# A two-layer token mixer on one core: in the delta rule's scan, two pairs of small products on TensorE are issued alternately, each pair in PSUM banks of its own, and ScalarE's copies stand in another order

## The chip, the cores and the metric

The kernel runs on one core of one Trainium2 chip, written in Bass: each engine (TensorE, VectorE, ScalarE, GpSimd, and SyncE for the DMAs) has its own instruction stream, and they are held together by semaphores that are written out by hand. The metric is the device time of one execution in microseconds (us). The kernel before has a median of 2457.78 us of 3 runs (2455.46 to 2459.18).

## What is computed

A trunk of two layers over 256 context tokens and 1024 latent tokens of width 1024. The even layer mixes an mLSTM branch and an RWKV-7 branch, the odd one an HGRN-2 branch and a long convolution. The change touches one function alone, the scan of the RWKV-7 branch, which runs in both directions over all 1280 tokens, with 8 heads of dimension 64. Cut to that part, the reference is:

```
def rwkv_scan(inputs, S):
    def step(S, xs):
        r, v, kk, w, k, a = xs
        sa = jnp.einsum('bhvk,bhk->bhv', S, -kk)
        S = S * w[:, :, None, :] + sa[..., None] * (kk * a)[:, :, None, :] + v[..., None] * k[:, :, None, :]
        return S, jnp.einsum('bhvk,bhk->bhv', S, r)

    S, ys = lax.scan(step, S, tuple(jnp.moveaxis(t, 2, 0) for t in inputs))
    return jnp.moveaxis(ys, 0, 2), S
```

## The kernel before

The scan (`stage_rwkv_scan`, from L1540) does not go token by token. It takes chunks of 64 tokens (C), 20 for each direction, 40 in all (N). Within a chunk the delta rule is a triangular system; its matrix is inverted by doubling, and the state passes from chunk to chunk. A **round** b (20 of them, B) inverts the matrices of the two chunks 2b and 2b+1, called lanes 0 and 1, and in the gaps of that work it carries the state through the two chunks of round b-1 and prepares those of round b+1. The 8 heads lie as 4 pairs (j), a pair's two heads (q) on the lower and the upper 64 partitions.

**The inversion** has five levels n (TOP = 5). Each is a ring through four engines' steps:

- `half_product(b, n)` (L1831, TensorE, 16 products of 64x64) into the pair banks 0 and 1; it waits for `merge_upper(b, n-1)`.
- `copy_half(b, n)` (L1901, ScalarE) copies the two banks to SBUF.
- `upper_product(b, n)` (L1840, TensorE, 16 products) waits for that copy and for `turn_inverse(b, n)` (L2045, L2047, VectorE, three 32x32 block transposes).
- `merge_upper(b, n)` (L2052, VectorE, a predicated copy of both banks) puts the result into the inverse, and then the next level's `half_product` may start.

While TensorE waits for a step of another engine, it does the work of the other rounds that its program puts there. In level 1 this is `begin_chunk(b-1, 0)` (L1787: the state times the first queries) and `strict_products(b+1, 0)` (L1730) ahead of the upper product, `solve_chunk(b-1, 0)` (L1796) and `begin_outputs(b-1, 0)` (L1805) behind it. Level 2 has `update` (L1813) and `end_outputs` (L1819) of lane 0 ahead, and `products(b+1, 0)` (L1741) behind. Levels 3 and 4 do the same for lane 1, with `begin_outputs` ahead of `solve_chunk`. Level 5 has `pull(b)` (L1778: both lanes, values times a part of the products) ahead, and `turn_keys` (L1753) and `turn_v` (L1768, transposes) behind.

All these products except `products`, `update`, `end_outputs` and the transposes use a quarter of TensorE: 64 rows by 64 columns. `strict_products`, `begin_chunk` and `solve_chunk` alternate between the two quarters in which rows and result lie in the same half (q, q); `pull` and `begin_outputs` use the two others. The half and upper products go through all four.

PSUM's eight banks in the scan: 0 and 1 the inversion, 2 and 5 the turned keys of the lanes, 3 and 4 `products` (4 also `turn_v`), 5 also `strict_products`, 6 (CHAIN) `pull`, `begin_chunk`, `solve_chunk` and `update`, 7 the outputs.

ScalarE's own order in a round is: `copy_keys` (L1905) of both lanes, half 1, values (L1912), outputs of two chunks back (L1941), u of lane 0 (L1924), half 2, values, strict of lane 0 (L1932, from bank 5 to `strict_t`), half 3, outputs, u of lane 1, strict of lane 1, half 4, half 5, `copy_pulled` (L1919). An engine takes its instructions in this order, whichever is ready first. `update` waits for the copied u, and `begin_chunk` for the copied pull.

GpSimd starts the next round's inverses (`begin_inverse`, L1988) from VectorE's masked products (`read_products`, L2037), and adds the second direction's outputs (L2000). SyncE loads the operands two rounds ahead, and weights of the next stage.

Of the kernel before, what the change touches and what calls it, by code (L numbers as in the profile page):

```python
# [19 lines left out]
P = 128  # L20
# [1519 lines left out]
def stage_rwkv_scan(p, arena, operands, v_dram, shared, spare, own, chunk_decay, y, next_weights, free, bonus_dram):  # L1540
# [55 lines left out]
    with ExitStack() as local:  # L1596
# [23 lines left out]
        PAIR, KEYS, TURN, STRICT, CHAIN, OUT = 0, (2, 5), 3, 5, 6, 7  # L1620
# [11 lines left out]
        with nc.Block() as block:  # L1632
# [88 lines left out]
            def _(pe):  # L1721
                def strict_products(b, lane):
                    s = 2 * b + lane
                    pe.wait_ge(operands_loaded[s % SLOTS], landed(s))
                    if s:
                        pe.wait_ge(strict_read, s)
                    if lane == 0 and b >= 2:
                        pe.wait_ge(keys_copied, 2 * (b - 1))
                    for j, q in both:
                        last = nc.tensor.matmul(bank(STRICT)[part(q), at(lane, j)], queries(s)[part(q), j, q, :],  # L1730
                                                keys(s)[part(q), j, q, :], start=True, stop=True)
                    last.then_inc(strict_ready, 1)

                def products(b, lane):
                    s = 2 * b + lane
                    if s:
# [8 lines left out]
                def turn_keys(b):  # L1745
                    for lane in range(2):
                        s = 2 * b + lane
                        if lane == 0 and b:
                            pe.wait_ge(keys_copied, 2 * b - 1)
                        if lane == 1:  # L1750
                            pe.wait_ge(strict_read, min(2 * (b + 2), N))
                        for j in range(J):
                            last = nc.tensor.transpose(bank(KEYS[lane])[:, j * P:(j + 1) * P],  # L1753
                                                       keys(s)[:, j].rearrange("p k t -> p (k t)"), p.const("ident"))
                        last.then_inc(keys_turned, 1)
# [16 lines left out]
                def pull(b):  # L1772
                    if b < WINDOWS:
                        pe.wait_ge(v_copied, 2 * (b + 1))
                    pe.wait_ge(state_ready, 2 * b + 1)
                    for lane in range(2):
                        for j, q in both:
                            last = nc.tensor.matmul(bank(CHAIN)[part(q), at(lane, j)], prod[part(1 - q), b % 2, lane, q, j, part(q)],  # L1778
                                                    uv(2 * b + lane)[part(1 - q), q, j, :], start=True, stop=True)
                    last.then_inc(pulled_ready, 1)  # L1780

# [9 lines left out]
                def solve_chunk(b, lane):  # L1791
                    s = 2 * b + lane
                    pe.wait_ge(rest_copied, s + 1)
                    pe.wait_ge(upper_merged, TOP * (b + 1))
                    for j, q in both:
                        last = nc.tensor.matmul(bank(CHAIN)[part(q), at(1, j)], own_inverse(b, lane, j, q), rest[part(q), j, :],  # L1796
                                                start=True, stop=True)
                    last.then_inc(u_summed, 1)

                def begin_outputs(b, lane):  # L1800
                    s = 2 * b + lane
                    if s:
                        pe.wait_ge(y_copied, s)
                    for j, q in both:
                        nc.tensor.matmul(bank(OUT)[part(1 - q), at(0, j)], queries(s)[part(q), j, 1 - q, :], state[part(q), j, :],  # L1805
                                         start=(j == 0), stop=False)
# [37 lines left out]
                for lane in range(2):  # L1844
                    strict_products(0, lane)
                    products(0, lane)
                turn_v(0)
                for b in range(B):
# [4 lines left out]
                    if ahead:  # L1853
                        strict_products(b + 1, 0)
                    upper_product(b, 1)
                    if before:
                        solve_chunk(b - 1, 0)
                        begin_outputs(b - 1, 0)
# [8 lines left out]
                    if ahead:  # L1867
                        strict_products(b + 1, 1)
                    if before:
                        begin_chunk(b - 1, 1)  # L1870
                    upper_product(b, 3)
                    if before:
                        begin_outputs(b - 1, 1)
                        solve_chunk(b - 1, 1)
# [8 lines left out]
                    pull(b)  # L1883
                    upper_product(b, 5)
                    turn_keys(b)
                    if b + 1 < WINDOWS:
                        turn_v(b + 1)
                for lane in range(2):
                    begin_chunk(B - 1, lane)
                    solve_chunk(B - 1, lane)  # L1890
                    begin_outputs(B - 1, lane)
                    update(B - 1, lane)
                    end_outputs(B - 1, lane)

            @block.scalar
            def _(act):
# [18 lines left out]
                def copy_pulled(b):  # L1915
                    act.wait_ge(pulled_ready, b + 1)
                    if b:
                        act.wait_ge(rest_copied, 2 * b)
                    nc.scalar.copy(flat(pulled[:, :, :, :]), narrow(bank(CHAIN))).then_inc(pulled_copied, 1)  # L1919
# [25 lines left out]
                for b in range(B):  # L1945
# [6 lines left out]
                    if b >= 2:  # L1952
                        copy_y(b - 2, 1)
# [7 lines left out]
                    if before:  # L1961
                        copy_y(b - 1, 0)
                        copy_u(b - 1, 1)
                    if ahead:
                        copy_strict(b + 1, 1)
                    copy_half(b, 4)
                    copy_half(b, 5)
# [3 lines left out]
                copy_y(B - 2, 1)  # L1971
# [1981 lines left out]
```

## Time and profile before

| | |
|---|---|
| median of 3 runs | 2457.78 us |
| span of the profiled execution | 2456.0 us (the median lies 1.8 us above it) |
| TensorE busy over the span | 2299.8 us, 94% |
| VectorE, ScalarE, GpSimd busy | 1340.4, 814.9, 250.8 us |
| the scan: first half product to last upper product | 926.5 to 1302.3 us |
| instruction queue of the whole kernel | 175 packets, 2.87 MB |

A profile page gives each engine's busy time, the groups of instructions by line and the chain that ended last. TensorE's records need care: each fp32 product of 64x64 stands in the trace as two LDWEIGHTS and two MATMUL records, so a group of 8 products shows as x16 and one of 16 as x32. A record's duration (some 0.22 us) is much longer than the distance to the next one, since products in different quarters overlap; what a group takes from TensorE is the distance from its first start to the first start of the next group. "issue" names idle time in which the engine waited for nothing that the profile shows.

### The profile page before, as it was taken

The numbers are of one execution on the slowest core, as the hardware profiler recorded it, in microseconds if no ns is written. First come the engines' busy times: TensorE is split into PE (matmuls) and PEld (weight loads), VectorE is DVE, ScalarE is ACT, GpSimd is POOL, SyncE is SP. The second block draws the span as 40 slices with busy tenths as digits, with TensorE's granted clock in tenths as the row PEclk, the third lists the DMA queues.
The fourth block names the chain that finished last, engine by engine and source line by source line (L and its number), as shares of the span: only waits on it lengthen the run. The fifth ranks groups of instructions, "written<-read, shape, count | busy, mean of one in ns | idle before, by whom it ended". The sixth has DMA issues, their size and how long they took to land. (4 is left out here: it accounts for less than half of the span.)

```text
span 2456.0 us, 50670 instructions
## 1 busy us (share of the span) xinstructions
PE 2299.8 (94%) x22140; PEld 1419.3 (58%) x22140; DVE 1340.4 (55%) x2181; ACT 814.9 (33%) x1533; POOL 250.8 (10%) x280
## 2 busy tenths in 40 slices
PE   6999999999989988988887998999998999999898
PEld 4444456666644447887784443444685666756443
DVE  3320335553348757777884454555395666667514
ACT  4121222224445653443342222110101445465311
POOL 0000000000002211111221102341100000000000
PEclk8999999999989999999998998999999999999999
DMA  8100122122055654433325432111122100000233
GB/s 332 60 19 7 43 78 76 63 65 71 22 154 144 170 155 117 118 91 93 96 58 194 128 109 76 47 47 34 69 102 82 36 27 27 27 18 10 96 97 116
DMA packets 131867, 207.29 MB, mean 84 GB/s; under 512 B 15630, under 2 KB 95246, under 8 KB 128063
## 3 DMA queue, kind: packets, MB, share of 16 engines
q1 hardware_dynamic: 118398, 154.74, 20.2%
q0 software_dynamic: 13248, 49.32, 7.0%
q8 instruction: 175, 2.87, 0.5%
q14 instruction: 46, 0.37, 0.0%
HBM read 154.01 MB, written 50.01 MB: 83 GB/s over the span
## 5 line engine op out<-in xcount | busy, mean ns | idle before, releaser
L737 PE MATMUL psum<-arena,shared 128*128 128x512 f32 (+1 forms) x864 | 328.7, 525 | 1.5 <-PEq L223 1.5
L2858 PE MATMUL psum<-arena,second_shared 128*128 128x512 f32 (+1 forms) x640 | 282.4, 568 | 11.0 <-PEq L3679 6.4
L737 PEld LDWEIGHTS psum<-arena,shared 128*128 128x128 f32 x864 | 157.0, 191 | 108.8 <-issue 101.8
L2858 PEld LDWEIGHTS psum<-arena,second_shared 128*128 128x128 f32 x640 | 112.5, 195 | 77.0 <-issue 71.8
L1243 PE MATMUL psum<-shared,arena 128*128 128x512 f32 x320 | 150.0, 617 | 0.0
L2244 PE MATMUL psum<-shared,fin_mix 128*128 128x512 f32 x320 | 143.4, 601 | 3.0 <-POOL fin_mix L2377 3.0
L1901 ACT COPY r_half<-psum 128x512 f32<-128x512 f32 x100 | 58.6, 586 | 151.1 <-PE psum L1831 151.0
L2244 PEld LDWEIGHTS psum<-shared,fin_mix 128*128 128x128 f32 x320 | 59.8, 192 | 75.0 <-issue 71.5
L1243 PEld LDWEIGHTS psum<-shared,arena 128*128 128x128 f32 x320 | 60.3, 196 | 73.4 <-issue 72.9
L841 ACT ACTIVATE shared<-psum 128x512 f32<-128x512 f32 (+1 forms) x48 | 25.2, 524 | 216.4 <-PE psum L737 216.4
L2052 DVE COPY_PREDICATED r_inv<-shared,psum 128x512 f32<-128x512 uint32 x100 | 73.4, 734 | 42.9 <-PE psum L1840 42.0
L2047 DVE STREAM_TRANSPOSE r_lower<-r_inv 64x256 f32<-64x256 f32 x200 | 88.0, 440 | 2.7
L1831 PE MATMUL psum<-r_inv,r_strict_t 64*64 64x64 f32 x3200 | 75.6, 226 | 14.2 <-issue 6.1
L1988 POOL TENSOR_TENSOR r_inv<-r_prod,shared 64x256 f32<-64x256 f32 x80 | 57.9, 724 | 289.1 <-PE psum L1796 188.5
L330 PE MATMUL psum<-arena,shared 128*128 128x512 f32 (+3 forms) x240 | 87.4, 523 | 0.0
L3143 DVE TENSOR_TENSOR arena<-arena,g_k 128x512 f32<-128x512 f32 x56 | 39.5, 706 | 87.4 <-ACT arena L3011 87.4
L1840 PE MATMUL psum<-r_half,r_lower 64*64 64x64 f32 x3200 | 75.3, 224 | 12.2 <-issue 8.9
L3011 ACT ACTIVATE arena<-arena 128x1024 f32<-128x1024 f32 x64 | 69.3, 1083 | 34.5 <-DVE arena L3124 32.8
L2849 PE MATMUL psum<-second_shared,arena 128*128 128x128 f32 x640 | 80.3, 277 | 0.0
L1831 PEld LDWEIGHTS psum<-r_inv,r_strict_t 64*64 64x64 f32 x3200 | 60.3, 135 | 29.0 <-issue 14.3
L2849 PEld LDWEIGHTS psum<-second_shared,arena 128*128 128x128 f32 x640 | 75.1, 192 | 1.1 <-issue 0.5
L3429 PE MATMUL psum<-arena,yf_weight 128*128 128x512 f32 x168 | 74.4, 592 | 0.0
(457 smaller groups left out, 4231.8 us busy)
## 6 DMA issues: line engine op xcount, KB each, us to landing
arena<-scratch_operands SPq DMA_DIRECT2D x152, 128.0 KB, 2.7
shared<-in_l_w_in SPq DMA_DIRECT2D x22, 512.0 KB, 4.0
scratch_spill<-shared POOLq DMA_DIRECT2D x16, 640.0 KB, 3.2
second_shared<-in_l_w_in SPq DMA_DIRECT2D x20, 512.0 KB, 3.8
scratch_operands<-arena POOLq DMA_DIRECT2D x14, 640.0 KB, 8.3
scratch_operands<-arena POOLq DMA_DIRECT2D x28, 320.0 KB, 11.2
shared<-in_l_mod_w SPq DMA_DIRECT2D x8, 1024.0 KB, 9.1
t_matrix<-in_transform SPq DMA_DIRECT2D x8, 1024.0 KB, 5.0
```

Of the source, the lines that this page charges most:

```text
L330: last = nc.tensor.matmul(p.psum[0:rows_out, bank_of[u], 0:width], lhsT, rhs, start=(k == 0), stop=(k == KT - 1))
L737: last = nc.tensor.matmul(p.psum[:, FILL + f % BANKS, 0:width], weight[:, q % PIECES, k, :], hT[:, k, at:at + width], start=(k == 0), stop ...
L1243: last = nc.tensor.matmul(p.psum[:, PROJECT + u % 2, :], hT[:, k, t * P:(t + 1) * P], weight[:, job, k, :], start=(k == 0), stop=(k == KT ...
L1831: last = nc.tensor.matmul(pair_bank(q, lane, jj)[part(r)], strict_t[part(q), b % 2, lane, 2 * jj + r, :], own_inverse(b, lane, 2 * jj + r, ...
L1840: last = nc.tensor.matmul(pair_bank(q ^ r, lane, jj)[part(q)], lower[part(r), q ^ r, four(lane, jj), :], half[part(r), q, four(lane, jj), ...
L2047: last = nc.vector.transpose(lower[part(1 - q), 1], here[part(q), 1])
L2052: nc.vector.copy_predicated(inv[:, b % 2].rearrange("p s l j n -> p s (l j) n"), added_to_pairs(direction(b), n), pair_banks.rearrange("p ...
L2244: last = nc.tensor.matmul(p.psum[:, OUT + 2 * (t % 2) + n, :], mixed[:, t % SLOTS, k, :], weight[:, k, n * BANK:(n + 1) * BANK], start=(k ...
L2849: last = nc.tensor.matmul(bank[:, (t - part[0]) * P:(t - part[0] + 1) * P], hT[:, kk, t * P:(t + 1) * P], w[:, kk, :], start=(kk == 0), st ...
L2858: last = nc.tensor.matmul(bank[:, 0:width], w[:, kk, :], hT[:, kk, first:first + width], start=(kk == 0), stop=(kk == KT - 1))
L3011: nc.scalar.activation(out, out, ACT.Exp).then_inc(sig["exps_ready"], 1)
L3429: last = nc.tensor.matmul(bank(made), left[:, k, :], right[:, k, :], start=(k == 0), stop=(k == HALF - 1))
```

## The change

Only `stage_rwkv_scan` is changed, in TensorE's and ScalarE's programs.

- `pull` gets bank 2 (PULL) in place of CHAIN, and the two keys' banks swap lanes. It is cut in lanes. `strict_and_pull(b, lane)` issues, for each pair of heads, two strict products of round b+1 and two pull products of round b in turn. Lane 0's stands in level 3, lane 1's in level 5, both between the half and the upper product. The strict products therefore leave level 1 (lane 0) and level 3 (lane 1), and half of the pull leaves level 5.
- `solve_and_begin_outputs` issues two products of the solve and two of the outputs' beginning in turn, in levels 1 and 3, behind the upper product.
- `turn_keys` is called by lanes, with `turn_v` between them; lane 1 waits for `copy_pulled`, whose bank it shares.
- The wait for the landed operands moves from the strict products to `products`, which is now the first reader.
- ScalarE: the copy of the outputs of lane 1 moves from the next round's level 1 to behind half 4; the strict copy of lane 1 moves from ahead of half 4 to behind half 5. The strict copy of lane 0 stays where it was, ahead of half 3. `copy_pulled` waits for both lanes' pulls and reads bank 2.

```diff
-        PAIR, KEYS, TURN, STRICT, CHAIN, OUT = 0, (2, 5), 3, 5, 6, 7
+        PAIR, KEYS, PULL, TURN, STRICT, CHAIN, OUT = 0, (5, 2), 2, 3, 5, 6, 7
...
+                def strict_and_pull(b, lane):
+                    if b + 1 < B:
+                        await_strict(b + 1, lane)
+                    if b < WINDOWS:
+                        pe.wait_ge(v_copied, 2 * b + lane + 1)
+                    if lane == 0 and b:
+                        pe.wait_ge(keys_copied, 2 * b)
+                    for j in range(J):
+                        if b + 1 < B:
+                            strict_product(2 * (b + 1) + lane, j, 0)
+                            strict = strict_product(2 * (b + 1) + lane, j, 1)
+                        pull_product(2 * b + lane, j, 1)
+                        pull = pull_product(2 * b + lane, j, 0)
+                    if b + 1 < B:
+                        strict.then_inc(strict_ready, 1)
+                    pull.then_inc(pulled_ready, 1)
...
-                def solve_chunk(b, lane):
+                def solve_and_begin_outputs(b, lane):
                     s = 2 * b + lane
                     pe.wait_ge(rest_copied, s + 1)
                     pe.wait_ge(upper_merged, TOP * (b + 1))
...
+                    for j in range(J):
+                        for q in range(2):
+                            last = nc.tensor.matmul(bank(CHAIN)[part(q), at(1, j)], own_inverse(b, lane, j, q), rest[part(q), j, :],
+                                                    start=True, stop=True)
+                        for q in (1, 0):
+                            nc.tensor.matmul(bank(OUT)[part(1 - q), at(0, j)], queries(s)[part(q), j, 1 - q, :], state[part(q), j, :],
+                                             start=(j == 0), stop=False)
+                    last.then_inc(u_summed, 1)
...
                     half_product(b, 1)
                     if before:
                         begin_chunk(b - 1, 0)
-                    if ahead:
-                        strict_products(b + 1, 0)
                     upper_product(b, 1)
                     if before:
-                        solve_chunk(b - 1, 0)
-                        begin_outputs(b - 1, 0)
+                        solve_and_begin_outputs(b - 1, 0)
...
                     half_product(b, 3)
-                    if ahead:
-                        strict_products(b + 1, 1)
                     if before:
                         begin_chunk(b - 1, 1)
+                    strict_and_pull(b, 0)
                     upper_product(b, 3)
                     if before:
-                        begin_outputs(b - 1, 1)
-                        solve_chunk(b - 1, 1)
+                        solve_and_begin_outputs(b - 1, 1)
...
                     half_product(b, 5)
-                    pull(b)
+                    strict_and_pull(b, 1)
                     upper_product(b, 5)
-                    turn_keys(b)
+                    turn_keys(b, 0)
                     if b + 1 < WINDOWS:
                         turn_v(b + 1)
+                    turn_keys(b, 1)
...
                     copy_half(b, 1)
                     copy_v(b, 0)
-                    if b >= 2:
-                        copy_y(b - 2, 1)
                     if before:
                         copy_u(b - 1, 0)
                     copy_half(b, 2)
...
                         copy_y(b - 1, 0)
                         copy_u(b - 1, 1)
+                    copy_half(b, 4)
+                    if before:
+                        copy_y(b - 1, 1)
+                    copy_half(b, 5)
                     if ahead:
                         copy_strict(b + 1, 1)
-                    copy_half(b, 4)
-                    copy_half(b, 5)
                     copy_pulled(b)
```

How the instructions stand now. TensorE, level 3 of a round and the start of level 4, before (L1831 half product, L1730 strict, L1787 begin_chunk, L1840 upper, L1805 outputs' beginning, L1796 solve):

```order
L1831 MATMUL psum<-r_inv,r_strict_t 64x64 x16
L1730 MATMUL psum<-arena 64x64 x8
L1787 MATMUL psum<-r_state,arena 64x64 x8
L1840 MATMUL psum<-r_half,r_lower 64x64 x16
L1805 MATMUL psum<-r_state,arena 64x64 x8
L1796 MATMUL psum<-r_rest,r_inv 64x64 x8
L1831 MATMUL psum<-r_inv,r_strict_t 64x64 x16
```

The same place in the changed kernel (L1845 half product, L1803 begin_chunk, L1723 strict, L1727 pull, L1854 upper, L1815 solve, L1818 outputs' beginning); the pairs of rows at L1723 and L1727, and those at L1815 and L1818, come four times each:

```order
L1845 MATMUL psum<-r_inv,r_strict_t 64x64 x16
L1803 MATMUL psum<-r_state,arena 64x64 x8
L1723 MATMUL psum<-arena 64x64 x2
L1727 MATMUL psum<-shared,r_prod 64x64 x2
...
L1854 MATMUL psum<-r_half,r_lower 64x64 x16
L1815 MATMUL psum<-r_rest,r_inv 64x64 x2
L1818 MATMUL psum<-r_state,arena 64x64 x2
```

The strict products of level 3 are now the next round's lane 0, where they were lane 1, and they stand behind begin_chunk, where they stood ahead of it.

ScalarE, from half 2 to the copy of the pull, before (L1901 half, L1912 values, L1932 strict, L1941 outputs, L1924 u, L1919 pulled):

```order
L1901 COPY r_half<-psum 128x512
L1912 COPY r_uv<-psum 64x256 x2
L1932 COPY r_strict_t<-psum 128x256
L1901 COPY r_half<-psum 128x512
L1941 COPY r_y<-psum 128x256
L1924 COPY r_uv<-psum 64x256 x2
L1932 COPY r_strict_t<-psum 128x256
L1901 COPY r_half<-psum 128x512 x2
L1919 COPY r_pulled<-psum 128x512
```

And now (L1910 half, L1921 values, L1941 strict, L1950 outputs, L1933 u, L1928 pulled):

```order
L1910 COPY r_half<-psum 128x512
L1921 COPY r_uv<-psum 64x256 x2
L1941 COPY r_strict_t<-psum 128x256
L1910 COPY r_half<-psum 128x512
L1950 COPY r_y<-psum 128x256
L1933 COPY r_uv<-psum 64x256 x2
L1910 COPY r_half<-psum 128x512
L1950 COPY r_y<-psum 128x256
L1910 COPY r_half<-psum 128x512
L1941 COPY r_strict_t<-psum 128x256
L1928 COPY r_pulled<-psum 128x512
```

The first strict copy keeps its place between half 2 and half 3, the second has moved behind half 5, and a copy of outputs stands between half 4 and half 5.

## Rows read from the trace of the kernel before

**Rows 1.** The page: the span and section 1, busy time by engine.
```profile
span 2456.0 us, 50670 instructions
...
PE 2299.8 (94%) x22140; PEld 1419.3 (58%) x22140; DVE 1340.4 (55%) x2181; ACT 814.9 (33%) x1533; POOL 250.8 (10%) x280
```

**Rows 2.** Busy time in stretches: start:end, length, busy us of PE, PEld, DVE, ACT, POOL, clock, DMA.
```profile
945.00:1300.00 355.00, 315.78 (x10960) 287.16 (x10957) 283.69 (x561) 147.42 (x334) 64.54 (x89) 1.00 0.33 91
```

**Rows 3.** Timeline of TensorE, one round: start, length, engine, line, count, idle before.
```profile
1040.08 0.69 PE L1831 MATMUL psum<-r_inv,r_strict_t 64*64 64x64 f32 x32
...
1047.50 0.69 PE L1831 MATMUL psum<-r_inv,r_strict_t 64*64 64x64 f32 x32
1048.01 0.63 PE L1730 MATMUL psum<-arena 64*64 64x64 f32 x16
1048.48 0.63 PE L1787 MATMUL psum<-r_state,arena 64*64 64x64 f32 x16
1048.99 0.69 PE L1840 MATMUL psum<-r_half,r_lower 64*64 64x64 f32 x32
1049.52 0.46 PE L1805 MATMUL psum<-r_state,arena 64*64 64x64 f32 x10
...
1050.53 0.69 PE L1831 MATMUL psum<-r_inv,r_strict_t 64*64 64x64 f32 x32
1051.39 0.69 PE L1813 MATMUL psum<-shared,r_k_tok 128*64 128x64 f32 x16 [0.17 <-ACT shared L1924]
...
1054.62 0.69 PE L1831 MATMUL psum<-r_inv,r_strict_t 64*64 64x64 f32 x32
1055.15 0.63 PE L1778 MATMUL psum<-shared,r_prod 64*64 64x64 f32 x16
1055.62 0.63 PE L1778 MATMUL psum<-r_uv,r_prod 64*64 64x64 f32 x16
1056.12 0.99 PE L1840 MATMUL psum<-r_half,r_lower 64*64 64x64 f32 x32
...
1058.50 0.69 PE L1831 MATMUL psum<-r_inv,r_strict_t 64*64 64x64 f32 x32
```

**Rows 4.** Timeline of ScalarE in levels 3 and 4 of the same round.
```profile
1048.26 0.58 ACT L1901 COPY r_half<-psum 128x512 f32<-128x512 f32 x1 [2.48 <-PE psum L1831]
1048.74 0.38 ACT L1941 COPY r_y<-psum 128x256 f32<-128x256 f32 x1
1050.50 0.75 ACT L1924 COPY shared<-psum 64x256 f32<-64x256 f32 x2 [1.38 <-PE psum L1796]
1051.27 0.37 ACT L1932 COPY r_strict_t<-psum 128x256 f32<-128x256 f32 x1
1051.54 0.59 ACT L1901 COPY r_half<-psum 128x512 f32<-128x512 f32 x1
```

**Rows 5.** Timeline of VectorE, the merge in level 3 of the same round.
```profile
1049.74 0.73 DVE L2052 COPY_PREDICATED r_inv<-shared,psum 128x512 f32<-128x512 uint32 x1
```

**Rows 6.** DMA queues, 945 to 1300 us: packets, MB, share of 16 engines.
```profile
q8 instruction: 86, 1.41, 1.7%
```

**Rows 7.** The same view, 1200.5 to 1227.2 us.
```profile
q8 instruction: 7, 0.11, 1.9%
```

**Rows 8.** Waits of TensorE, 926 to 1302 us: in total, times, longest.
```profile
PE psum L1840 <- issue: 8.9, 11, 2.0
PE psum L1831 <- issue: 6.1, 12, 0.9
PE psum L1813 <- issue: 4.9, 6, 1.5
PE psum L1805 <- issue: 3.7, 4, 1.7
PE psum L1796 <- issue: 2.4, 2, 1.6
```

More of the change, by code:

```diff
@@ L1721, in _, with strict_product, pull_product, await_strict @@
             def _(pe):
-                def strict_products(b, lane):
+                def strict_product(s, j, q):
+                    return nc.tensor.matmul(bank(STRICT)[part(q), at(s % 2, j)], queries(s)[part(q), j, q, :],
+                                            keys(s)[part(q), j, q, :], start=True, stop=True)
+                def pull_product(s, j, q):
+                    return nc.tensor.matmul(bank(PULL)[part(q), at(s % 2, j)], prod[part(1 - q), s // 2 % 2, s % 2, q, j, part(q)],
+                                            uv(s)[part(1 - q), q, j, :], start=True, stop=True)
+                def await_strict(b, lane):
                     s = 2 * b + lane
-                    pe.wait_ge(operands_loaded[s % SLOTS], landed(s))
                     if s:
@@ L1727, in strict_products @@
                     if lane == 0 and b >= 2:
-                        pe.wait_ge(keys_copied, 2 * (b - 1))
+                        pe.wait_ge(keys_copied, 2 * (b - 2) + 1)
+                def strict_products(b, lane):
+                    await_strict(b, lane)
                     for j, q in both:
-                        last = nc.tensor.matmul(bank(STRICT)[part(q), at(lane, j)], queries(s)[part(q), j, q, :],
-                                                keys(s)[part(q), j, q, :], start=True, stop=True)
+                        last = strict_product(2 * b + lane, j, q)
                     last.then_inc(strict_ready, 1)
+                def strict_and_pull(b, lane):
[14 more added lines that the diff above has]
+                    pull.then_inc(pulled_ready, 1)
                 def products(b, lane):
                     s = 2 * b + lane
+                    pe.wait_ge(operands_loaded[s % SLOTS], landed(s))
                     if s:
@@ L1743, in products, with turn_keys @@
                     last.then_inc(products_ready, 1)
[L1745 to L1755, printed above, removed]
+                def turn_keys(b, lane):
+                    s = 2 * b + lane
+                    if lane == 0:
+                        pe.wait_ge(strict_read, min(2 * (b + 2), N))
+                    if lane == 1:
+                        pe.wait_ge(pulled_copied, b + 1)
+                    for j in range(J):
+                        last = nc.tensor.transpose(bank(KEYS[lane])[:, j * P:(j + 1) * P],
+                                                   keys(s)[:, j].rearrange("p k t -> p (k t)"), p.const("ident"))
+                    last.then_inc(keys_turned, 1)
                 def turn_v(w):
@@ L1770, in turn_v @@
                     last.then_inc(v_turned, 1)
[L1772 to L1780, printed above, removed]
                 def begin_chunk(b, lane):
@@ L1794, in solve_chunk @@
                     pe.wait_ge(upper_merged, TOP * (b + 1))
[L1795 to L1801, printed above, removed]
                     if s:
                         pe.wait_ge(y_copied, s)
-                    for j, q in both:
-                        nc.tensor.matmul(bank(OUT)[part(1 - q), at(0, j)], queries(s)[part(q), j, 1 - q, :], state[part(q), j, :],
-                                         start=(j == 0), stop=False)
+                    for j in range(J):
+                        for q in range(2):
[5 more added lines that the diff above has]
+                    last.then_inc(u_summed, 1)
                 def update(b, lane):
@@ L1844, in _ @@
                 for lane in range(2):
+                    products(0, lane)
                     strict_products(0, lane)
-                    products(0, lane)
                 turn_v(0)
@@ L1882, in _ @@
                     half_product(b, 5)
-                    pull(b)
+                    strict_and_pull(b, 1)
                     upper_product(b, 5)
-                    turn_keys(b)
+                    turn_keys(b, 0)
                     if b + 1 < WINDOWS:
                         turn_v(b + 1)
+                    turn_keys(b, 1)
                 for lane in range(2):
                     begin_chunk(B - 1, lane)
-                    solve_chunk(B - 1, lane)
-                    begin_outputs(B - 1, lane)
+                    solve_and_begin_outputs(B - 1, lane)
                     update(B - 1, lane)
@@ L1915, in copy_pulled @@
                 def copy_pulled(b):
-                    act.wait_ge(pulled_ready, b + 1)
+                    act.wait_ge(pulled_ready, 2 * (b + 1))
                     if b:
                         act.wait_ge(rest_copied, 2 * b)
-                    nc.scalar.copy(flat(pulled[:, :, :, :]), narrow(bank(CHAIN))).then_inc(pulled_copied, 1)
+                    nc.scalar.copy(flat(pulled[:, :, :, :]), narrow(bank(PULL))).then_inc(pulled_copied, 1)
                 def copy_u(b, lane):
@@ L1970, in _ @@
                 copy_keys(B - 1, 1)
-                copy_y(B - 2, 1)
                 for lane in range(2):
```

## The prediction

> **What bounds the kernel now.** The page first: TensorE is busy for 94% of the span [rows 1]. That share does not say what its work is worth, because the change touches one stage only. The stretches give that stage: 315.8 us of 355 busy on TensorE and 283.7 on VectorE, at full clock, so 39 us of TensorE are idle and VectorE has 71 us to spare [rows 2]. A busy time of overlapped records is not a queue, though, so I read one round of the timeline.
>
> A round takes 18.42 us (1040.08 to 1058.50, both half products of level 1) [rows 3], and there are 20. Look at level 3. The half product starts at 1047.50, the upper at 1048.99, the next half product at 1050.53. Between half and upper stand 0.51 us of the half product itself, 0.47 of the strict products and 0.51 of begin_chunk, 1.49 in all. The other side of the same interval is ScalarE's copy: it starts at 1048.26, 0.76 after the half product, takes 0.58 [rows 4], and the upper product starts 0.15 after its end, again 1.49. The two are equal: the filling work is as long as the wait that it covers. Behind the upper product the merge starts at 1049.74 and takes 0.73 [rows 5], and the half product of level 4 follows 0.06 later. That makes 1.54, with 0.53 for the upper product and 1.01 for outputs and solve, which fill it. So the level is bound by the ring half, copy, upper, merge, **1.49 + 1.54 = 3.03 us**, and the filling work only just fits.
>
> The second thing that bounds is idle time put down to "issue". Its five largest rows give 8.9 + 6.1 + 4.9 + 3.7 + 2.4 = **26.0 us** in the scan [rows 8]. What it is shows in the instruction queue: 86 packets in 355 us [rows 6], while TensorE executed 10960 + 10957 records [rows 2], 255 for a packet. In a stretch of 26.7 us there were 7 packets [rows 7], one in 3.8 us, and the mean is 4.1. TensorE thus uses up its program nearly as fast as it arrives, and where it runs ahead, it stands.
>
> The Trainium skill, Advanced Engine Details and Errata, section on the ISA cache, has an instruction line of 16 KB or 256 instructions, two lines only. The 255 records for a packet agree with it.
>
> **The change part by part.**
>
> 1. Alternation. A group that uses two quarters of TensorE takes 0.47 us for 16 records (strict, 1048.01 to 1048.48; one lane's pull, 1055.15 to 1055.62). One that uses all four takes 0.51 to 0.53 for 32 (half, upper) [rows 3]. I price the new mixed groups like the latter. Each saves 0.94 - 0.53 = 0.41 us of TensorE's queue. There are 19 x 2 of strict with pull and 20 x 2 of solve with outputs, 78 x 0.41 = 32.0 us. **On the path this is worth 0 directly.** In levels 1 and 3 the 1.54 us from upper to half are set by the merge, in level 5 the 1.49 from half to upper by ScalarE's copy (1054.62 to 1056.12 [rows 3]), and shorter filling leaves TensorE waiting there. Level 1 has begin_chunk alone ahead of its upper product, 0.98 us of work in a wait of 1.49. What the shorter filling can give is cover for stalls, part 4.
>
> The Trainium skill, TensorEngine Tiling (Array Packing), says under Key Properties that different tiles can load weights and multiply in parallel, up to four of 64x64. By that rule alone the sum would be -32 us; rows 3 agree with the rate, not with the path.
>
> 2. ScalarE's order, level 3. This is the term that decides. The strict product of lane 0 moves from level 1 to level 3 on TensorE, but ScalarE's copy of it still stands between half 2 and half 3. ScalarE now has to wait, in level 3, for products that are issued *behind* the half product whose copy is next in its queue. From the half product's start H: 0.51 half, 0.51 begin_chunk, then the mixed group, whose last strict product starts about 0.48 later; 0.25 from last product to copy (half product: last start H + 0.51, copy H + 0.76). The strict copy starts at H + 1.75. The half copy can start 0.27 behind it (1051.27 to 1051.54 [rows 4]), at H + 2.02, and the upper product comes 0.73 after that (1048.26 to 1048.99), at **H + 2.75 in place of H + 1.49: +1.26 us**. Queued behind that copy on ScalarE are the outputs' and u's copies, behind it on TensorE the upper product and everything after; VectorE's merge waits too. 18 rounds at 1.26, and the first, without begin_chunk, at 0.75: **+23.4 us**.
>
> 3. u of lane 1. In level 3 the outputs' beginning stood ahead of the solve, so u's copy began 0.98 us after the first of them (1049.52 to 1050.50), and the update waited 0.17 us for it (1051.39) [rows 3, 4]. In the mixed group the last solve product starts at 0.46, the copy at 0.71, 0.27 earlier. The update can start at 1051.12 instead, just behind the half product (1050.53 + 0.51). 19 x 0.27 = **-5.1 us**. For lane 0 the solve stood first already: 0. The strict copy that leaves level 4 (1051.27) had delayed the half copy there by some 0.3 us, which the update and end_outputs covered: 0.
>
> 4. Stalls for instructions. The number of records is the same, so packets are too. But a TensorE that waits in level 3 for 1.26 us gives the next packet time to arrive, and a stall of up to 0.4 to 0.5 us in a shortened filling is covered by the ring's wait. Bounds: nothing of the 26.0 us goes, or all of it. Against all of it: more than half (8.9 + 6.1) stands before the half and the upper products themselves, where nothing covers a stall, and denser groups use up a packet sooner. I take a third: **-8.7 us**.
>
> 5. At nothing: the keys' turn in two parts, whose second waits for the pull's copy (from level 5's half product 0.76 to the copy, 0.59 + 0.37 + 0.59 for half, strict, pull: H + 2.4, while the next half product comes at H + 3.88). If the turned keys come late, the next half copy does, by at most 0.1 us in ten rounds, 1 us. The outputs' copy of lane 1, between half 4 and half 5, 0.38 us [rows 4] in a gap of nearly 3 us. The moved wait for operands: they are loaded two rounds ahead. No DMA is added or passed.
>
> Sum: 23.4 - 5.1 - 8.7 = **+9.6 us**, against the profiled execution's 2456.0 us (1.8 below the median): 2465.6 there, 2467.4 as a median. A measurement of this kernel can tell 0.2%, 4.9 us, from no change.
>
> **The rivals.**
>
> - *Instructions set the pace* (no change). If the scan takes what its packets take, then the wait in level 3 falls into time in which TensorE would have stood anyway. For: 3.8 us a packet in a stretch and 4.1 on average. Against: rings at exactly 3.03 us exist, which are not paced by packets. It needs 18.3 of the 26.0 us of stalls to be covered: 2458. The page of the Trainium skill named above (Advanced Engine Details and Errata, ISA cache), with its two lines of 256 instructions, speaks for this one.
> - *All stalls covered* (faster). The same mechanism beyond its balance: from 18.3 us covered upward the kernel gains. Its place are the shortened groups of levels 1, 3 and 5 and the pause in level 3. With all 26.0 covered: 18.3 - 26.0 = -7.7, 2450.
> - *TensorE's queue is the bound* (faster). Then 78 x 0.41 us come off, and ScalarE's wait is small beside them: 2457.8 - 32.0 = 2426. Against: the equal 1.49 us by copy and by filling. This is what the tiling page's rule, taken alone, would give.
> - *Nothing is covered* (slower still). The stalls stay where they are, because each packet's fetch starts later by the wait: 2457.8 + 18.3 = 2476, and with the keys' 1 us 2477.
>
> **How the numbers follow.** Forecast, 2461 to 2473: 0.50. Instructions set the pace, near 2458: 0.20. All stalls covered, 2450: 0.14. TensorE's queue, 2426: 0.03. Nothing covered, 2476: 0.13. From these, faster by more than 4.9 us 0.17, slower 0.62, within 0.21; some of the forecast's lower edge is counted as same, some of the second case as slower. The range goes from 2450 to 2478 and leaves out the queue's case and the tails.
>
> **What would show it.** In the changed profile: level 3's half to upper product at 2.6 to 2.9 us in nearly every round (1.49 before), with ScalarE's half copy of that level starting right behind the strict copy, and its idle time ahead of the strict copy put down to L1723. Levels 1 and 5 at 1.49 from half to upper. The mixed groups at 0.51 to 0.55 us. The update of lane 1 without a wait for u. "issue" rows together at 14 to 20 us. TensorE's busy time in the scan lower by 20 us or more although the span is not. The forecast is wrong if level 3 stays at 1.5 us, or if the issue rows fall below 8 us; a round then takes less than 18.4 us.

## The result and the profile after

The changed kernel takes 2470.54 us (median of 4 runs, 2467.05 to 2473.84), the kernel before 2458.48 beside it (median of 4). The ratio is 1.0055, 95% interval 1.0043 to 1.0068: **slower by 12 to 14 us**. The forecast was 2467.4 within 2450 to 2478.

The profiled execution has a span of 2471.9 us, 15.9 above that of before [rows 1]. It belongs to the slowest of the four runs (2473.84), so sizes read from it are a little large. The page of the changed kernel:

```profile
span 2471.9 us, 50688 instructions
...
PE 2284.6 (92%) x22140; PEld 1397.9 (57%) x22140; DVE 1338.6 (54%) x2181; ACT 814.9 (33%) x1533; POOL 250.9 (10%) x280
```

TensorE has 15 us less busy time and the kernel is 16 us longer: what overlap saved has become idle time, and more. Where? The timeline of TensorE and ScalarE, level 3 of one round (compare [rows 3, 4]):

```profile
1069.51 0.69 PE L1845 MATMUL psum<-r_inv,r_strict_t 64*64 64x64 f32 x32
1070.02 0.57 PE L1803 MATMUL psum<-r_state,arena 64*64 64x64 f32 x14
...
1071.17 0.37 ACT L1941 COPY r_strict_t<-psum 128x256 f32<-128x256 f32 x1 [3.04 <-PE psum L1723]
...
1071.44 0.59 ACT L1910 COPY r_half<-psum 128x512 f32<-128x512 f32 x1
1071.91 0.39 ACT L1950 COPY r_y<-psum 128x256 f32<-128x256 f32 x1
1072.17 0.69 PE L1854 MATMUL psum<-r_half,r_lower 64*64 64x64 f32 x32 [1.05 <-ACT r_half L1910]
```

The half product starts at 1069.51. ScalarE stands for 3.04 us until the strict products (L1723) are there, copies them at 1071.17, and only then the half product's result, at 1071.44. The upper product comes at 1072.17, 2.66 us after the half product, where it was 1.49. TensorE waited 1.05 us before it. The waits of the scan (926 to 1325 us), as in [rows 8], with ScalarE's and the weight loads' rows:

```profile
ACT r_strict_t L1941 <- PE psum L1723: 76.9, 22, 4.8
...
PE psum L1854 <- ACT r_half L1910: 32.9, 55, 1.1
...
PEld psum L1854 <- DVE r_lower L2055: 18.2, 42, 1.0
...
PE psum L1845 <- DVE r_inv L2060: 14.5, 34, 0.8
...
PE psum L1845 <- issue: 5.7, 8, 1.4
...
PE psum L1833 <- issue: 4.2, 6, 1.0
PE psum L1818 <- issue: 3.3, 2, 1.9
PE psum L1854 <- issue: 3.2, 7, 1.0
...
PE psum L1827 <- issue: 1.8, 2, 1.0
PE psum L1803 <- issue: 1.8, 2, 1.2
PE psum L1815 <- issue: 1.6, 2, 1.4
```

The first row is the cause: ScalarE waits for strict products in front of the half copy. The second holds its cost on TensorE, 19.7 us of it in level 3, in 19 waits; most of the other 13 us are waits of levels 1 and 5, where TensorE now has less to do ahead of the upper product. The issue rows sum to 23.0 us with two of 0.7 that are not shown; the same sum of before, with its small rows, is 28.5.

The table is worked out from the first starts of the half and upper products in the two timelines: mean distances in us over rounds 2 to 20.

| level | before, half to upper | upper to half | after, half to upper | upper to half |
|---|---|---|---|---|
| 1 | 1.55 | 2.05 | 1.56 | 1.76 |
| 2 | 2.23 | 1.89 | 2.39 | 1.88 |
| 3 | 1.61 | 1.71 | **2.78** | 1.58 |
| 4 | 2.32 | 1.81 | 2.21 | 1.87 |
| 5 | 1.58 | 2.14 | 1.52 | 2.13 |

Level 3's first part grew by 1.17 us, 22 us over 19 rounds; levels 1 and 3, behind the upper product, gave back 0.4 a round. The whole table adds up to 0.79 us a round, 15.0 in 19 rounds. One thing stands outside it: the first round took 23.33 us where it took 18.38. With it the scan takes 20.1 us more (395.4 against 375.3), and the span only 15.9, because the scan begins 4.0 us earlier (922.5 against 926.5), behind stages that the change does not touch. The stretches 922 to 945 us, before and then after (the seventh number is the granted clock, as in [rows 2]):

```profile
922.00:945.00 23.00, 16.78 (x460) 14.67 (x460) 15.05 (x29) 6.90 (x15) 5.76 (x8) 0.85 0.43 124
```

```profile
910.50:922.00 11.50, 6.77 (x67) 6.03 (x68) 2.85 (x5) 0.74 (x2) 2.54 (x4) 0.50 0.59 151
922.00:945.00 23.00, 17.90 (x425) 15.65 (x424) 12.49 (x24) 5.53 (x12) 3.23 (x5) 0.51 0.27 89
```

In the changed kernel TensorE ran at the lower of its two levels, 1.2 GHz, through nearly the whole first round, and did fewer products in the same time. It stood there already in the 11.5 us ahead of the scan, the first row.

### The profile page after: what moved, and what is told of

It reads as the page before. It is cut to its first block and busy times, and to the rows that moved or that the text cites. A ratio compares the mean times of both kernels' runs of the same rounds, so it can differ in the third digit from the quotient of the medians.

```text
span 2471.9 us, 50688 instructions
## 1 busy us (share of the span) xinstructions
PE 2284.6 (92%) x22140; PEld 1397.9 (57%) x22140; DVE 1338.6 (54%) x2181; ACT 814.9 (33%) x1533; POOL 250.9 (10%) x280
## 3 DMA queue, kind: packets, MB, share of 16 engines
q1 hardware_dynamic: 118398, 154.74, 20.1%
## 5 line engine op out<-in xcount | busy, mean ns | idle before, releaser
L1854 PE MATMUL psum<-r_half,r_lower 64*64 64x64 f32 x3200 | 76.6, 231 | 37.4 <-ACT r_half L1910 33.7
L1845 PE MATMUL psum<-r_inv,r_strict_t 64*64 64x64 f32 x3200 | 77.4, 232 | 23.3 <-DVE r_inv L2060 14.5
L1854 PEld LDWEIGHTS psum<-r_half,r_lower 64*64 64x64 f32 x3200 | 62.9, 141 | 48.3 <-issue 26.7
L1910 ACT COPY r_half<-psum 128x512 f32<-128x512 f32 x100 | 58.7, 587 | 85.0 <-PE psum L1845 83.7
L1845 PEld LDWEIGHTS psum<-r_inv,r_strict_t 64*64 64x64 f32 x3200 | 61.8, 140 | 39.3 <-DVE r_inv L2060 20.3
L3019 ACT ACTIVATE arena<-arena 128x1024 f32<-128x1024 f32 x64 | 69.3, 1083 | 34.6 <-DVE arena L3132 32.8
```

Of the source, the lines that this page charges most:

```text
L1845: last = nc.tensor.matmul(pair_bank(q, lane, jj)[part(r)], strict_t[part(q), b % 2, lane, 2 * jj + r, :], own_inverse(b, lane, 2 * jj + r, ...
L1854: last = nc.tensor.matmul(pair_bank(q ^ r, lane, jj)[part(q)], lower[part(r), q ^ r, four(lane, jj), :], half[part(r), q, four(lane, jj), ...
L1910: nc.scalar.copy(half[:, :, :, :].rearrange("p q f n -> p q (f n)"), pair_banks).then_inc(half_copied, 1)
L3019: nc.scalar.activation(out, out, ACT.Exp).then_inc(sig["exps_ready"], 1)
```

## The experiments

Each kernel was timed beside the kernel before, whose medians in the three sets were 2457.1, 2456.5 and 2456.5 us. Differences from before are given by the ratio, times 2457 us.

### ScalarE's strict copy, moved

```diff
                     copy_v(b, 1)
-                    if ahead:
-                        copy_strict(b + 1, 0)
                     copy_half(b, 3)
+                    if ahead:
+                        copy_strict(b + 1, 0)
                     if before:
                         copy_y(b - 1, 0)
```

> The changed kernel with one edit: ScalarE's copy of lane 0's strict products stands behind the half copy of level 3, where it stood ahead of it. Theory (ScalarE's order costs the time): half to upper product of level 3 falls from 2.67 us back to 1.49, 18 rounds of 1.18 us, -21 us, less what stalls for instructions take back (a third to a half of that): 2450 to 2458 us, at or below the kernel before. Rival (instructions arrive at a fixed pace and set the time): the issue rows grow by what the level loses, 2466 to 2471 us. Rival (the first round at half clock, 23.3 us against 18.4, is most of the loss): 2466 us, with the first round still at 23 us.

Measured: 2464.61 us, ratio 1.0037 (1.0024 to 1.0051), +9 us on before. Level 3 is down from 2.78 to 1.66 us, and still only 4 to 6 of the 21 us came back. Level 4's half to upper product rose from 2.21 to 2.71, level 3's upper to half from 1.58 to 1.93. The waits of TensorE in this kernel say why:

```profile
PE psum L1845 <- issue: 11.4, 15, 1.4
...
PE psum L1833 <- issue: 7.7, 9, 1.7
PE psum L1854 <- issue: 5.0, 11, 0.9
...
PE psum L1815 <- ACT r_y L1950: 2.0, 7, 0.3
```

All issue rows together are 32.8 us, against 23.0. And there is a new wait: the joined solve (L1815) needs the outputs copied (L1950), which now queue behind the strict copy. The first expectation failed in its size. The next kernel takes the new wait away (half 3, outputs, strict, u).

```diff
-                    if ahead:
-                        copy_strict(b + 1, 0)
                     copy_half(b, 3)
                     if before:
                         copy_y(b - 1, 0)
+                    if ahead:
+                        copy_strict(b + 1, 0)
+                    if before:
                         copy_u(b - 1, 1)
```

> The changed kernel with ScalarE's copy of lane 0's strict products between the outputs' copy and u's copy of level 3: half 3, outputs, strict, u. Theory (the first try moved the wait: the alternated solve of level 3 needs the outputs copied, and that copy stood behind the strict one, 0.3 us late in 7 rounds, with the update of level 4 behind it): level 3 at 1.49 us and the wait of the solve for the outputs' copy gone, another -3 to -6 us, 2459 to 2462 us. Rival (what the moved copy gave back was taken by stalls for instructions alone): as the first try, 2463 to 2466 us.

Measured: 2462.82 us, ratio 1.0029 (1.0019 to 1.0040), +7 us; against the changed kernel -6 to -8 us. The rival is as near as the theory: issue rows are 32.8 us here too. So ScalarE's order costs 6 to 8 us net in the alternated kernels, of 21 that it costs in level 3.

### The alternation, undone

```diff
-                    for j in range(J):
-                        if b + 1 < B:
+                    if b + 1 < B:
+                        for j in range(J):
                             strict_product(2 * (b + 1) + lane, j, 0)
                             strict = strict_product(2 * (b + 1) + lane, j, 1)
+                    for j in range(J):
                         pull_product(2 * b + lane, j, 1)
...
+                    for j in range(J):
                         for q in (1, 0):
                             nc.tensor.matmul(bank(OUT)[part(1 - q), at(0, j)], queries(s)[part(q), j, 1 - q, :], state[part(q), j, :],
```

> The changed kernel with the pairs of products in sequence again, in the same places and banks: first all strict products, then the pull; first the solve, then the outputs' beginning. Theory (the alternation lies under waits of the ring): TensorE's queue is 78 x 0.41 = 32 us longer, the time rises by 0 to 6 us; in level 3 the strict products come out 0.2 us sooner and the copy with them, -4 us: 2465 to 2475 us. Rival (TensorE's queue is the bound): 2490 to 2502 us.

Measured: 2467.55 us, ratio 1.0044 (1.0029 to 1.0059), 3 us below the changed kernel (the intervals overlap). A queue that is 32 us longer costs nothing. That rules out the rival in which TensorE's queue is the bound. The same edit on top of the mended copy order:

> As the run before this one, and the pairs of products in sequence again. Theory (a TensorE that has less to do between the ring's steps loses granted clock, so the alternation costs a little and gives nothing): first round below 20 us, no drop of the clock in mid-scan, 3 us below the alternated one, 2456 to 2460 us. Rival (once ScalarE's order is out of the way, TensorE's queue is the bound and the alternation pays): 5 to 15 us slower than the alternated one.

Measured: 2458.03 us, ratio 1.0004 (0.9995 to 1.0013), no different from before, and below the alternated kernel beside it by 4.8 us (medians) or 6.1 (ratios). Moving strict products and pull to their new levels and banks is thus free within 0.13%; alternating both pairs costs. The stretches of the first round, alternated, then in sequence:

```profile
922.00:945.00 23.00, 18.26 (x470) 16.05 (x472) 13.50 (x26) 6.81 (x15) 3.76 (x6) 0.65 0.32 95
```

```profile
922.00:945.00 23.00, 17.36 (x459) 15.21 (x456) 14.17 (x27) 6.48 (x14) 4.45 (x7) 0.78 0.38 114
```

One profile each is thin evidence for a clock. How thin it is shows in the last experiment's kernel (2456.18 us), which differs from the kernel before only in the order of VectorE's instructions:

```profile
922.00:945.00 23.00, 18.47 (x436) 16.42 (x437) 14.23 (x27) 6.56 (x14) 4.34 (x6) 0.64 0.28 86
```

Its first round took 20.65 us, and one of 21.45 us stands in a kernel without any alternation (the one with more instructions, below). A slow first round alone is thus no sign of the alternation. The mean granted clock of every run says more.

| kernel | runs | mean granted clock |
|---|---|---|
| before (first, second, third set) | 25, 23, 29 | 0.9728, 0.9738, 0.9733 |
| changed | 4 | 0.9705 |
| strict copy behind half 3, both alternated | 8 | 0.9711 |
| changed, none alternated | 6 | 0.9722 |
| mended order, both alternated | 8 | 0.9704 |
| the same, first round kept busy | 10 | 0.9717 |
| changed, first round kept busy | 5 | 0.9718 |
| mended order, none alternated | 12 | 0.9730 |
| mended order, strict with pull alone | 12 | 0.9726 |
| before with the solve alternated | 12 | 0.9728 |

At two levels, 1 and 0.5, a mean of c over 2457 us is 2 x (1 - c) x 2457 us at the lower one: 145 to 146 us for both alternated, 133 for none, so 13 us more. Before gives 129 to 134 by its three sets. The kernels with more or fewer instructions and the two variants of before without alternation lie at 0.9730 to 0.9741.

### One alternation at a time

> The same kernel with strict products and pull alternated, the solve and the outputs' beginning in sequence. It tells which alternation costs the 5 us between the two kernels of the last set. Theory (both thin TensorE out; in the kernel before, the solve's alternation alone cost nothing measurable, so the limit is passed only by the two together): 2458 to 2461 us, between the two. Rival (strict with pull alone does it, by its place in the first round): 2462 to 2463 us, half clock in the first round.

```diff
                         for q in range(2):
                             last = nc.tensor.matmul(bank(CHAIN)[part(q), at(1, j)], own_inverse(b, lane, j, q), rest[part(q), j, :],
                                                     start=True, stop=True)
+                    for j in range(J):
                         for q in (1, 0):
```

Measured: 2458.15 us, ratio 1.0006 (0.9995 to 1.0016). The other one, put alone into the kernel before:

```diff
                     if before:
-                        solve_chunk(b - 1, 0)
-                        begin_outputs(b - 1, 0)
+                        solve_and_begin_outputs(b - 1, 0)
```

> The kernel before with one part of the change: the solve and the outputs' beginning alternate, for both lanes. Theory (the merge sets the 1.54 us from upper to half product in levels 1 and 3): -3 to -8 us, from the earlier u copy of lane 1 and from stalls that now lie under the wait, 2450 to 2456 us. Rival (TensorE's queue is the bound): 40 x 0.41 = -16 us, 2442 us. Rival (instructions set the pace): no change, 2458 us.

Measured: 2458.39 us, ratio 1.0010 (0.9995 to 1.0024): no change, as instructions at a fixed pace would have it and against the 3 to 8 us that I expected, and no clock lost. Strict with pull alone is free in the mended kernel; both alternations together cost it 5 to 6 us and 13 us of full clock. The solve's alternation alone was measured only in the kernel before, where up to 5.9 us lie inside its interval. Whether it needs the other one to cost something in the mended kernel, no run shows.

### ScalarE's other moves

```diff
-                    if ahead:
-                        copy_strict(b + 1, 1)
                     copy_half(b, 4)
+                    if before:
+                        copy_y(b - 1, 1)
                     copy_half(b, 5)
+                    if ahead:
+                        copy_strict(b + 1, 1)
```

> The kernel before with ScalarE's part of the change alone: lane 1's outputs copied behind half 4, lane 1's strict products behind half 5. Theory (these two copies lie beside other work in either place): no change, 2456 to 2460 us. Rival (the strict copy ahead of half 4 held level 4 up by 0.3 us a round): -5 us, 2453 us.

Measured: 2458.57 us, ratio 1.0001 (0.9988 to 1.0013). Free in the kernel before, as the prediction had it.

### A busier first round

```diff
+                def keep_busy(b):
+                    if b == 0:
+                        for j, q in both:
+                            nc.tensor.matmul(bank(CHAIN)[part(q), at(0, j)], queries(0)[part(q), j, q, :],
+                                             keys(0)[part(q), j, q, :], start=True, stop=True)
...
                     half_product(b, 1)
+                    keep_busy(b)
```

(the same behind upper 1, half 2, upper 3 and half 4), in the mended kernel and in the changed one.

> As the first run of this set, with 5 groups of 8 products added in the first round, in places where TensorE only waits there (their results are not read). Theory (TensorE stands at half clock through the first round because it has too little to do there): the first round falls from 21 to 23 us to 18 to 20 us though it holds more work, -2 to -4 us in all. Rival (the clock is low there for what came before the scan, whatever the scan does): the added products take their time at half clock, first round 23 us or more, 0 to +3 us.

> The changed kernel with the same 5 groups of products added in the first round. Theory (sparse first round keeps the clock at half): first round from 23.3 to about 19.5 us, 2466 to 2468 us. Rival: 2470 to 2473 us.

Measured: 2461.43 us (1.0027, 1.0014 to 1.0040) and 2473.21 us (1.0069, 1.0057 to 1.0081). The first rounds fell, from 21.22 to 17.30 us and from 23.33 to 20.62, with more work in them. The times did not follow: -1.4 us, inside the noise, and +2.7. The mean granted clock rose, from 0.9704 to 0.9717 and from 0.9705 to 0.9718, by about half of what the alternation had taken. Single runs of a kernel scatter by 0.001 to 0.002, so this rise is barely clear of noise, but no time came back with it. The profiled execution of the first shows the lower clock six more times, between 959 and 1290 us, 3.4 us each, but it is the slowest of its ten runs (2471.15 us). So the slow first round is not what the alternation costs, and that the lower clock is the reason for its 3 to 6 us is not shown.

### More instructions, and fewer

Two kernels test what the issue rows are. Both start from the mended kernel without alternation (2458.0 us). One issues begin_chunk of level 1 twice, in a place where the ring leaves half a microsecond free; the other leaves out the outputs' beginning.

```diff
-                    for j, q in both:
+                    for j, q in both * (2 if lane == 0 else 1):
                         last = nc.tensor.matmul(bank(CHAIN)[part(q), at(0, j)], queries(s)[part(q), j, q, :], state[part(q), j, :],
```

> The kernel without alternation and with ScalarE's copy order mended (2458.0 us), with begin_chunk of level 1 issued twice into the same place: 8 products or 32 more records a round, 0.47 us of TensorE's queue in a place where the ring leaves 0.51 us free. Theory (instructions arrive at 3.8 to 4 us a packet, and the stalls are TensorE running ahead of them): 0.13 packet more a round, up to 0.5 us, 19 rounds: +4 to +9 us, 5 packets more. Rival (stalls have another cause, and work under the ring's wait is free): -1 to +2 us.

```diff
-                    for j in range(J):
-                        for q in (1, 0):
-                            nc.tensor.matmul(bank(OUT)[part(1 - q), at(0, j)], queries(s)[part(q), j, 1 - q, :], state[part(q), j, :],
-                                             start=(j == 0), stop=False)
```

> The same kernel with the outputs' beginning left out (the state's part of the outputs is missing from the result): 64 records of TensorE fewer in each lane pair, 5% of a round, in places where the merge sets the time. Theory (instruction supply): 10 packets of 16 KB fewer over the kernel is the most, 5 expected; stalls drop by a third to a half, -8 to -15 us, 2443 to 2450 us, less if the clock falls. Rival (work under the ring's wait is free and its instructions too): 2456 to 2459 us.

The pages, with more and then with fewer instructions (the whole kernel; before and in the mended kernel without alternation, 175 packets):

```profile
span 2457.9 us, 51328 instructions
...
q8 instruction: 178, 2.92, 0.5%
```

```profile
span 2445.5 us, 49408 instructions
...
q8 instruction: 170, 2.79, 0.5%
```

Measured: 2462.59 us (1.0023, 1.0014 to 1.0031) and 2447.24 us (0.9958, 0.9946 to 0.9970). Three packets more cost 4.6 us, five fewer gave back 10.8, both in places where TensorE has time: **2.2 us a packet** for the fewer and at most 1.5 for the more. My expectation of 5 more packets was wrong (640 records are 2.5), the time was right.

The kernel with fewer is the clean one of the two. Its issue rows fell from 31.1 us in the kernel between to 20.9, nearly all of the 10.8. With more instructions they did not rise (30.1). There the second begin_chunk also delays the solve of level 1, which starts 0.65 us behind the upper product where it was 0.49, up to 3 us in 19 rounds, so its 4.6 us are not the packets' alone. Two waits of the kernel with fewer:

```profile
PE psum L1843 <- DVE r_inv L2059: 17.0, 38, 0.9
...
PE psum L1843 <- issue: 6.7, 12, 1.2
```

The half product now waits for the merge 38 times (11 times and 4.7 us in the kernel between): the ring shows again where the stalls had covered it.

That the issue rows are TensorE running out of instructions stands in the traces themselves. The kernel before has 22 stalls of over 0.5 us in the scan. Counted in TensorE's records, the distance from one to the next is always a multiple of 252.7, to within 4 records, which is close to the 255 of a packet, and each stall ends 2.2 to 3.1 us after a packet starts on the instruction queue. The same holds for the 28 such stalls of the kernel between.

The Trainium skill, Advanced Engine Details and Errata, section on the ISA cache, gives a 16 KB line of 256 instructions. Five packets for the 1280 records left out agree with it.

### Level 4's floor

```diff
-                    if ahead:
-                        read_products(b + 1, 0, 1)
                     turn_inverse(b, 4)
+                    if ahead:
+                        read_products(b + 1, 0, 1)
```

> The kernel before with one masked product of VectorE (lane 0, second head) behind the block transposes of level 4, where it stood ahead of them. Theory (level 4 cannot go below 1.83 us from half to upper product because the transposes come late, 0.12 us above level 2's 1.71): floor of level 4 at 1.71 us, 0 to -2.5 us, 2454 to 2457 us. Rival (stalls for instructions fill what is gained): no change.

Measured: 2456.18 us, ratio 0.9998 (0.9990 to 1.0007): no change. Level 4 keeps its 1.95 us in rounds without a stall, so in the kernel before the place of this product was not its limit. No kernel of the study that computes everything beats the one before.

## Why the prediction was right, and where its steps were off

**Direction and size held** (+9.6 forecast, +12 to +14 measured). The main mechanism is the forecast one. That the size came so near is in part luck: three smaller terms were off, in both directions.

- Part 2, ScalarE's order, +23.4 us: the mechanism and its place are shown. Half to upper product in level 3 is 2.67 us in the rounds without a stall (2.75 forecast), 22 us in all. The first idle row names L1723, as forecast.
- Part 4, the stalls, -8.7 us: mis-sized. Taking ScalarE's wait away gives 6 to 8 us net in the alternated kernels and 9.5 in those in sequence (2467.55 to 2458.03), so 12 to 15 of the 21 to 22 us were covered, not a third of 26.0. The issue rows show the larger part of it: 23.0 us with the wait, 32.8 without. Against the kernel before they fell by only 5.5, because the moved products brought stalls of their own (31.1 us in the mended kernel in sequence, 28.5 before). So the 14 to 20 us of issue rows that were to show the forecast did not come. My reason for a third was that most stalls stand before half and upper products. As I read it now, it missed that a pause anywhere in a packet's records lets the next one arrive; no run tests this by itself.
- Part 3, u of lane 1, -5.1 us: the copy does come earlier, but level 4 stops at 1.83 us, where the weight load of the upper product waits for the block transposes (10 times, 2.4 us of the row of 18.2 above; most of that row lies in levels 1 and 5). Level 4 had stood at 1.95, so the term is 19 x 0.12 = -2.3 us. The prediction had not looked at what comes next after u.
- Part 1, alternation, 0: right about the queue, shown by the kernels without it. It is not 0 in total: the two together cost 3 to 6 us, and the prediction had no term for it. The lower clock goes with the alternation in the means of 4 to 12 runs. But where the mean clock rose by half of that again, no time came back, so the cause of this cost stays open. TensorE's busy time in the scan fell by 13 us (331.8 to 318.9), not by 20 or more as forecast.
- Part 5, at nothing: the copy order alone, in the kernel before, and the new levels and banks with the mended order measured no difference.

From the kernel before to the changed one the ratios give 1.0 us for the moves, 9.8 for ScalarE's order and 2.7 for the alternation, 13.5 in all. By the other way, the alternation first, they are 1.0, 6.1 and 6.4. Both ways end at the same two kernels, so they add up by construction and are no test of their parts.

Of the rivals, "instructions set the pace" was half right: it is what covered most of the new wait. "TensorE's queue" is out.

## What to carry to other kernels

When a producer's instructions move on one engine, move the consumer's in the other engine's list too: an in-order copy that stands ahead of a step on the ring waits for whatever was moved behind it. Packing work closer gives nothing where a ring of other engines sets the interval; look first at what releases the next step. And where many small products run through TensorE, count instructions: leaving out 64 records a round gave 11 us, in a kernel that computes less, and shortening the queue by 32 us gave nothing.

## What the runs showed of the hardware

- A group of 16 records over two quarters of TensorE takes 0.47 us, one of 32 over four 0.51 to 0.53 [rows 3]. In the mixed groups of the changed kernel 0.43 to 0.52 us lie between the first start and the last.
- The instruction stream limits TensorE in the scan: one packet for some 255 records, 3.8 us apart in a dense stretch [rows 7], and stalls at distances that are multiples of some 253 records. Five packets fewer gave 10.8 us, though TensorE waited for others in the places they came from.
- The mean granted clock of the whole kernel was lower with both alternations: 0.9704 against 0.9730. In the stretch of the first round it was 0.51 in the changed kernel and 0.85 in the one before, but 0.64 also in a kernel without alternation.
